# Hybrid decoder trunk on one core: sums of down-projection weight blocks formed by adding DMA transfers instead of VectorE

## The chip, the cores and the metric

One Trainium2 chip, one core of it. The metric is the device time of one launch in microseconds (us). The kernel before takes 1595.86 us, the median of three runs that lie between 1595.35 and 1596.35 us.

## The reference, cut to what matters

Two layers of a decoder trunk over 512 tokens of width 1024. The change is in the second half of each layer, the MLP:

```python
for l in range(DEPTH):                      # DEPTH = 2
    ...                                     # norm, projections, conv / gated linear attention / window attention, w_o
    h = rms_norm(x, norm2_w[l])
    x = x + jnp.square(jax.nn.relu(h @ w_up[l])) @ w_down[l]     # w_up (1024, 4096), w_down (4096, 1024)
```

All is float32. The output is x, (1, 512, 1024).

## The kernel before, in words

**Precision by splitting.** Each operand of a TensorE product is kept as a high part (rounded by ScalarE) and a low part (what is left, by VectorE), and each product is three matmuls: high by high, high by low, low by high. A *unit* is a block of weights, 128 x 1024 numbers, that is split so: `split_high` (ScalarE, L803 to L820, 128x1024 copy), then `split_low` (VectorE, L1037 to L1045). There are four buffers for split units (`SPLIT = 4`), so the split of unit n waits until TensorE has finished unit n-4 (`unit_done`, L816).

**The MLP.** It runs in four quarters of 1024 hidden columns. A quarter is eight units `up` (hidden = up projection, ReLU and square on ScalarE) and then fourteen units `dn` (down projection). The down projection of a quarter is a product of a 512x1024 and a 1024x1024 matrix, each seen as 2x2 blocks: Strassen's scheme in Winograd's form, seven block products instead of eight, from sums of blocks of the hidden values and sums of blocks of w_down. Each product is two units: `pair` 0 and 1 are two halves of its 512 contraction rows, so `dn(14q + 2*place + pair)` is one unit, of twelve matmuls 128x512. The seven products run in the order `PRODUCT = (0, 4, 5, 2, 3, 1, 6)`: place 0 is product 0, place 1 is product 4, and so on.

**The weight blocks.** For each pair the blocks b11, b12, b21, b22 of a quarter (128 x 1024 numbers each, 512 KB) are loaded into a buffer `down[pair]` (`raw_down`) by two DMAs issued by SyncE (L493), and `down_full[pair]` says that they are there. VectorE then forms the sums in place, four instructions for each pair and quarter, `ta`, `tb`, `tc`, `td`: b12 = b22 - b12 (L1493), b11 = b12 + b11 (L1495), b22 = b22 - b11 (L1499), b21 = b21 - b11 (L1497). `split_high` of a unit waits for the sum that it reads (L811). Each sum overwrites a block whose earlier value must have been split before. Products 0, 1 and 5 read blocks as loaded. When the last of a quarter's units of a pair are split, `down_free[pair]` allows SyncE to load the next quarter.

**Order of the work.** The four engines' orders in the MLP are lists written out: `PE_LATE`, `ACT_LATE` (ScalarE) and `DVE_LATE` (VectorE); a word with `+` is the split of a unit, `rs` takes a product out of PSUM, `fo` folds sums of products into x, `su`/`sh`/`sl`, `df`/`dh`/`dl` and `hh`/`hl` prepare the hidden values, `RM` is the norm's factors, `ra`, `rb` add the w_o product. Every engine works through its list strictly in order. GpSimd has no block in this kernel. After the last quarter, layer 1's first steps (`UT4` to `UT7`: transposes of x on TensorE; `gq0`, `gq1`, `gk0`) follow in the same lists, and after layer 1 the output is stored.

The sums of products g1, g5, g6, g7 (`product_sums`, L1415, L1417) collect over the quarters; `fold` (L1419 to L1430) and `scaled_into_x` (L1395) bring them into x with the factor `rsq2`.

Of the kernel before, what the change touches and what calls it, by code (L numbers as in the profile page):

```python
# [10 lines left out]
P = 128  # L11
# [78 lines left out]
ACT_LATE = """+wa3 +wb0 +wb1 V0 +wb2 +wb3 V1 V2 V3 +up0 +up1 sq0 +up2 V4 V5 sq1 V6 +up3 V7 sq2 sq3 +up4 rl0 rl1 hh0 +up5 +up6 rl2  # L90
hh1 hh2 rl3 +up7 dh0 rl4 +dn0 hh3 sh0 hh4 rl5 +dn1 hh5 rl6 sh1 +dn2 hh6 rl7 +dn3 sh2 sh3 +dn4 +dn5 hh7 +dn6 +dn7 +dn8
+dn9 +dn10 +dn11 +dn12 +dn13 +up8 +up9 +up10 +up11 rl8 hh8 +up12 rl9 rl10 hh9 +up13 hh10 +up14 rl11 +up15 hh11 dh1
rl12 +dn14 hh12 sh4 +dn15 rl13 hh13 rl14 sh5 +dn16 sh6 rl15 +dn17 +dn18 sh7 hh14 +dn19 +dn20 hh15 +dn21 +dn22 +dn23
+dn24 +dn25 +dn26 +dn27 +up16 +up17 +up18 +up19 rl16 +up20 hh16 rl17 rl18 hh17 hh18 +up21 +up22 +up23 rl19 hh19 dh2
rl20 +dn28 sh8 hh20 +dn29 rl21 sh9 rl22 hh21 +dn30 hh22 rl23 +dn31 +dn32 sh10 +dn33 sh11 +dn34 +dn35 +dn36 +dn37 +dn38
+dn39 hh23 +dn40 +dn41 +up24 +up25 +up26 rl24 +up27 hh24 rl25 hh25 +up28 +up29 +up30 rl26 rl27 hh26 +up31 hh27 dh3
rl28 +dn42 hh28 sh12 rl29 +dn43 hh29 sh13 +dn44 rl30 hh30 sh14 rl31 +dn45 hh31 sh15 +dn46 +dn47 +dn48 +dn49 +dn50
+dn51 +dn52 +dn53 +dn54 +dn55 +gq0 UT4 +gq1 UT5 UT6 +gk0 UT7""".split()


DVE_LATE = """+wa3 ra0 +wb0 ra1 +wb1 ra2 ra3 V0 +wb2 +wb3 V1 +up0 V2 +up1 V3 rb0 ta0 rb1 rb2 +up2 rb3 +up3 V4 V5 V6 V7 +up4 RM hl0
+up5 +up6 ta1 df0 +up7 hl1 hl2 dl0 su0 +dn0 tb0 hl3 hl4 su1 +dn1 hl5 tb1 su2 +dn2 sl0 sl1 su3 hl6 +dn3 sl2 rs0 +dn4
rs1 sl3 +dn5 +dn6 rs2 td0 +dn7 rs3 +dn8 td1 rs5 rs4 +dn9 rs6 rs7 hl7 +dn10 tc0 +dn11 rs8 +dn12 tc1 rs9 +dn13 rs10 +up8
+up9 +up10 +up11 rs11 rs13 hl8 ta2 rs12 +up12 +up13 ta3 hl9 df1 hl10 +up14 +up15 dl1 su4 +dn14 hl11 tb2 +dn15 sl4 hl12
tb3 su5 hl13 su6 +dn16 sl5 sl6 su7 +dn17 +dn18 td2 rs15 rs14 +dn19 sl7 td3 +dn20 rs16 rs17 hl14 rs18 +dn21 rs19 +dn22
hl15 +dn23 +dn24 rs21 rs20 tc2 rs22 +dn25 tc3 +dn26 rs23 +dn27 +up16 rs24 rs25 rs27 +up17 ta4 rs26 +up18 +up19 ta5
hl16 +up20 hl17 hl18 +up21 +up22 df2 +up23 hl19 dl2 su8 sl8 +dn28 tb4 su9 +dn29 tb5 su10 sl9 hl20 hl21 hl22 +dn30 su11
+dn31 sl10 +dn32 rs29 +dn33 rs28 td4 sl11 rs30 +dn34 +dn35 rs31 rs33 rs32 td5 +dn36 +dn37 +dn38 rs35 rs34 tc4 +dn39
hl23 tc5 rs36 +dn40 rs37 +dn41 rs38 +up24 +up25 rs39 +up26 fo7 ta6 rs41 +up27 rs40 +up28 fo6 hl24 +up29 +up30 hl25 ta7
df3 +up31 hl26 hl27 dl3 su12 +dn42 hl28 sl12 tb6 su13 +dn43 sl13 tb7 +dn44 su14 hl29 hl30 sl14 su15 +dn45 hl31 sl15  # L110
rs42 rs43 +dn46 fo1 +dn47 rs44 rs45 +dn48 td6 +dn49 td7 rs46 +dn50 +dn51 rs47 rs49 +dn52 +dn53 tc6 rs48 fo3 fo4 fo2
rs50 rs51 tc7 +dn54 fo0 +dn55 UT4 +gq0 rs52 UT5 UT6 rs53 UT7 +gq1 fo5 rs54 rs55 +gk0""".split()
# [89 lines left out]
def hybrid_trunk(nc, x, x_cols, positions, params, w_in, gla_wa2, w_branch, w_o, w_up, w_down, norms, consts, gmask, out):  # L202
# [3 lines left out]
    with ctx:  # L206
# [101 lines left out]
        rsq2 = after("rsqrt_tokens_mlp_sq", [TT])  # L308
        ident, ones = cst[:, 0:P], cst[:, CC["ones"]:CC["ones"] + 1]
# [10 lines left out]
        def sem(name):  # L320
            return ctx.enter_context(nc.semaphore(name))
# [9 lines left out]
        down_free = [sem(f"down_free{i}") for i in range(PAIRS)]  # L331
        acc_free = [sem(f"acc_free{i}") for i in range(4)]
# [7 lines left out]
         diff_ready, b12_summed, b11_summed, b21_summed, b22_summed, angle_ready, sines_ready, first_full, first_hi, first_lo) = map(sem, """  # L340
# [6 lines left out]
         diff_ready b12_summed b11_summed b21_summed b22_summed angle_ready sines_ready first_full first_hi first_lo""".split())  # L347
# [442 lines left out]
        def _(act):  # L790
# [69 lines left out]
            for l in range(DEPTH):  # L860
# [125 lines left out]
                for word in ACT_LATE:  # L986
# [16 lines left out]
                    elif kind == "rl":  # L1003
                        a, free = done(act, l, f"up{i}")
                        nc.scalar.activation(hid[:, k, :], a[:], ACT.Relu).then_inc(free, 1)  # L1005
                        nc.scalar.drain()
                        nc.scalar.activation(hid[:, k, :], hid[:, k, :], ACT.Square).then_inc(hid_val, 1)
                    elif kind == "hh":
                        if k < BK:
                            nc.scalar.activation(h11[0][:, k, :], hid[:, k, 0:2 * P], ACT.Copy).then_inc(hid_hi, 1)  # L1010
                        else:
                            nc.scalar.activation(h2[0][:, k - BK, :], hid[:, k, :], ACT.Copy).then_inc(hid_hi, 1)
                    elif kind == "dh":
                        act.wait_ge(diff_val, l * QUARTERS + i + 1)
                        nc.scalar.activation(hd[0][:], hd_sum[:], ACT.Copy).then_inc(diff_hi, 1)
                    elif kind == "sh":
                        act.wait_ge(sums_val, l * QUARTERS * BK + i + 1)
                        nc.scalar.activation(hs[0][:, i % BK], hs_sum[:, i % BK], ACT.Copy).then_inc(sums_hi, 1)


        @block.vector
        def _(dve):
# [120 lines left out]
            for l in range(DEPTH):  # L1143
# [249 lines left out]
                def scaled_into_x(row, t, half, part):  # L1393
                    x_at = x_tok[:, 2 * row + t, half * SEQ:(half + 1) * SEQ]
                    return V.scalar_tensor_tensor(out=x_at, in0=part, scalar=rsq2[:, 2 * row + t:2 * row + t + 1], in1=x_at,  # L1395
# [23 lines left out]
                def fold(i):  # L1419

                    g1, g6, g5, g7 = (g[:] for g in gsum)
                    if i == 1:
                        V.tensor_tensor(g6, g6, g1, ALU.add)
                    elif i == 3:
                        V.tensor_tensor(g7, g7, g6, ALU.add)
                    else:
                        row, half, part = {0: (0, 0, g1), 2: (0, 1, g6), 4: (1, 1, g7), 5: (1, 0, g7),
                                           6: (0, 1, g5), 7: (1, 1, g5)}[i]
                        for t in range(2):
                            scaled_into_x(row, t, half, part[:, t, :])  # L1430

                for word in DVE_LATE:
# [21 lines left out]
                    elif kind == "RM":  # L1454
                        row_norm(2 * l + 1, rsq2[:])
                        V.tensor_tensor(rsq2[:], rsq2[:], rsq2[:], ALU.mult)
                    elif kind == "hl":
# [8 lines left out]
                    elif kind == "df":  # L1466
                        dve.wait_ge(hid_val, (l * QUARTERS + i) * 8 + BK)
                        V.tensor_tensor(hd_sum[:], hid[:, 0:BK, 0:2 * P], hid[:, 0:BK, 2 * P:],
# [4 lines left out]
                    elif kind == "su":  # L1473
# [13 lines left out]
                    elif kind in ("ta", "tb", "tc", "td"):  # L1487
                        n, pair = l * QUARTERS + i // 2, i % 2
                        b11, b12 = down[pair][:, :, 0, 0:SEQ], down[pair][:, :, 0, SEQ:]
                        b21, b22 = down[pair][:, :, 1, 0:SEQ], down[pair][:, :, 1, SEQ:]  # L1490
                        if kind == "ta":
                            dve.wait_ge(down_full[pair], (n + 1) * 32)
                            V.tensor_tensor(b12, b22, b12, ALU.subtract).then_inc(b12_summed, 1)  # L1493
                        elif kind == "tb":
                            V.tensor_tensor(b11, b12, b11, ALU.add).then_inc(b11_summed, 1)  # L1495
                        elif kind == "tc":
                            V.tensor_tensor(b21, b21, b11, ALU.subtract).then_inc(b21_summed, 1)  # L1497
                        else:
                            V.tensor_tensor(b22, b22, b11, ALU.subtract).then_inc(b22_summed, 1)  # L1499
# [57 lines left out]
```

## Time and profile before

| | |
|---|---|
| runs | 1595.86 us median (1595.35 to 1596.35) |
| the profiled execution | 1595.84 us, of which the span from the first to the last instruction is 1594.0 us |
| TensorE (PE) busy | 1568.7 us, 98% |
| VectorE (DVE) busy | 1077.5 us, 68% |
| ScalarE (ACT) busy | 743.9 us, 47% |
| GpSimd (POOL) busy | 0.2 us |
| mean DMA rate | 96 GB/s, 153.23 MB in all |

PE is TensorE's matmuls, PEld its weight loads. An engine's busy time says little of what ends last; the waits of PE do, since PE is nearly always at work. Matmuls overlap in the records (one lasts 0.39 us and the next starts 0.23 us after it), so a pause between records is a little shorter than the time that is lost. SPq, DVEq mean the instruction queue of an engine (DMA issues, drains, semaphores).

### The profile page before, as it was taken

How to read it: one execution, taken by the hardware profiler on the slowest of the kernel's cores; microseconds unless marked ns; L12 is line 12 of the kernel's file. 1: busy time of each engine (PE TensorE's matmuls, PEld its weight loads, DVE VectorE, ACT ScalarE, POOL GpSimd, SP SyncE). 2: the span in 40 equal slices, each digit the busy share in tenths (PEclk: the TensorE clock that was granted, in tenths of full speed). 3: DMA queues.
4: the chain of work that ended last, by engine and by line, in shares of the span. 5: the costliest groups of instructions: out<-in, count | busy, mean ns of one | idle time of the engine just before them, and what ended most of it. 6: DMA issues, size and time to landing. Idle time of an engine off the chain costs nothing.

```text
span 1594.0 us, 21259 instructions
## 1 busy us (share of the span) xinstructions
PE 1568.7 (98%) x7528; PEld 1283.7 (81%) x7528; DVE 1077.5 (68%) x1511; ACT 743.9 (47%) x1131; POOL 0.2 (0%) x4
## 2 busy tenths in 40 slices
PE   8999999999999999999999999999999999999997
PEld 7877778888888888888777787788888888888885
DVE  5577764555458878687966777555455586877788
ACT  5657552323247363636345566422232563636361
POOL 0000000000000000000000000000000000000000
PEclk9999999999999999999999999999999999999999
DMA  7321312332261322323023212133323514141401
GB/s 230 105 80 55 96 63 80 106 114 98 79 212 53 139 73 100 112 105 112 1 82 103 81 54 80 54 106 113 99 80 106 185 53 159 54 158 53 159 1 53
DMA packets 109321, 153.23 MB, mean 96 GB/s; under 512 B 5120, under 2 KB 81440, under 8 KB 109216
## 3 DMA queue, kind: packets, MB, share of 16 engines
q1 hardware_dynamic: 108496, 151.27, 28.7%
q8 instruction: 60, 0.98, 0.2%
q10 hardware_dynamic: 720, 0.61, 0.1%
q14 instruction: 45, 0.37, 0.1%
HBM read 149.77 MB, written 2.10 MB: 95 GB/s over the span
## 4 chain that ended last, share of the span: by engine, by line
PE 86%; DVE 9%; ACT 2%; DVEq 1%; issue 1%; DMA 1%; SPq 0%; ACTq 0%
PE acc L538 18%; PE acc L539 18%; PE acc L540 18%; PE acc L589 5%; PE acc L590 5%; PE acc L591 5%; PE acc L560 4%; PE acc L562 4%; PE acc L561 4%; DVE wl_rows L1042 3%; DVE x_tokens L1395 1%; PE bank L726 1%; PE bank L745 1%; PE bank L737 1%; DMA raw<-in_w_in_dram 1%
## 5 line engine op out<-in xcount | busy, mean ns | idle before, releaser
L538 PE MATMUL acc<-uh,wh 128*128 128x512 f32 x1152 | 453.5, 394 | 6.4 <-DVEq L1136 4.5
L540 PE MATMUL acc<-uh,wl 128*128 128x512 f32 x1152 | 449.3, 390 | 0.0
L539 PE MATMUL acc<-ul,wh 128*128 128x512 f32 x1152 | 449.3, 390 | 0.0
L538 PEld LDWEIGHTS acc<-uh,wh 128*128 128x128 f32 x1152 | 216.7, 188 | 58.1 <-issue 5.6
L540 PEld LDWEIGHTS acc<-uh,wl 128*128 128x128 f32 x1152 | 216.7, 188 | 45.9
L539 PEld LDWEIGHTS acc<-ul,wh 128*128 128x128 f32 x1152 | 216.9, 188 | 43.7
L1042 DVE TENSOR_TENSOR wl<-raw,wh 128x1024 fp32r<-128x1024 f32 x142 | 174.0, 1225 | 73.1 <-ACT wh L820 61.1
L820 ACT ACTIVATE wh<-raw 128x1024 fp32r<-128x1024 f32 x142 | 150.6, 1060 | 134.8 <-PE acc L540 98.0
L820 ACT ACTIVATE wh_rows<-raw_down 128x1024 fp32r<-128x1024 f32 x112 | 118.9, 1062 | 155.5 <-DVE raw_down L1497 66.7
L1042 DVE TENSOR_TENSOR wl_rows<-raw_down,wh_rows 128x1024 fp32r<-128x1024 f32 x112 | 137.2, 1225 | 11.1 <-ACT wh_rows L820 1.1
L1072 DVE TENSOR_TENSOR gate_tanh<-acc,rsqrt_rows 128x512 f32<-128x512 f32 x48 | 33.2, 691 | 116.6 <-PE acc L540 116.4
L980 ACT ACTIVATE gate_tanh<-gate_tanh 128x512 f32<-128x512 f32 x40 | 25.3, 633 | 171.7 <-DVEq L1073 171.7
L560 PE MATMUL acc<-wh_rows,uh 128*128 128x512 f32 (+1 forms) x256 | 96.0, 375 | 0.6 <-DVE gla_a_tokens L1165 0.6
L562 PE MATMUL acc<-wl_rows,uh 128*128 128x512 f32 (+1 forms) x256 | 93.4, 365 | 0.0
L561 PE MATMUL acc<-wh_rows,ul 128*128 128x512 f32 (+1 forms) x256 | 93.3, 364 | 0.0
L589 PE MATMUL acc<-wh_rows,hidden_hi 128*128 128x512 f32 x192 | 75.7, 394 | 7.4 <-DVE wl_rows L1042 5.0
L1005 ACT ACTIVATE hidden<-acc 128x512 f32<-128x512 f32 x64 | 38.3, 599 | 95.0 <-PE acc L540 93.3
L589 PE MATMUL acc<-wh_rows,hidden_sums_hi 128*128 128x512 f32 x192 | 75.1, 391 | 0.3 <-DVE x_tokens L1395 0.3
L590 PE MATMUL acc<-wh_rows,hidden_lo 128*128 128x512 f32 x192 | 75.2, 392 | 0.0
L591 PE MATMUL acc<-wl_rows,hidden_hi 128*128 128x512 f32 x192 | 75.2, 392 | 0.0
L590 PE MATMUL acc<-wh_rows,hidden_sums_lo 128*128 128x512 f32 x192 | 74.8, 389 | 0.0
L591 PE MATMUL acc<-wl_rows,hidden_sums_hi 128*128 128x512 f32 x192 | 74.7, 389 | 0.0
(227 smaller groups left out, 2378.9 us busy)
## 6 DMA issues: line engine op xcount, KB each, us to landing
raw<-in_w_in_dram SPq DMA_DIRECT2D x39, 1024.0 KB, 5.2
raw<-in_w_up_dram SPq DMA_DIRECT2D x32, 1024.0 KB, 5.6
raw_down<-in_w_down_dram SPq DMA_DIRECT2D x32, 1024.0 KB, 8.2
raw_branch<-in_w_in_dram SPq DMA_DIRECT2D x12, 1024.0 KB, 5.0
raw_branch<-in_w_branch_dram SPq DMA_DIRECT2D x12, 1024.0 KB, 5.1
raw_branch<-in_w_o_dram SPq DMA_DIRECT2D x8, 1024.0 KB, 5.0
x_tokens<-in_x_dram SPq DMA_DIRECT2D x8, 256.0 KB, 8.2
raw_kv<-in_w_in_dram SPq DMA_DIRECT2D x4, 512.0 KB, 4.9
```

Source lines behind the costliest of these rows:

```text
L538: nc.tensor.matmul(a[:], wh[slot][:, k, :], right_h, start=at_k == 0, stop=False)
L539: nc.tensor.matmul(a[:], wh[slot][:, k, :], right_l, start=False, stop=False)
L540: last = nc.tensor.matmul(a[:], wl[slot][:, k, :], right_h, start=False, stop=at_k == n - 1)
L560: nc.tensor.matmul(to, left_h[:, k, s], h[:, row, 0:cols], start=k == 0, stop=False)
L561: nc.tensor.matmul(to, left_l[:, k, s], h[:, row, 0:cols], start=False, stop=False)
L562: last = nc.tensor.matmul(to, left_h[:, k, s], lo[:, row, 0:cols], start=False, stop=k == KT - 1)
L589: nc.tensor.matmul(to[:], left[0], h[:, row, :], start=k == 0, stop=False)
L590: nc.tensor.matmul(to[:], left[1], h[:, row, :], start=False, stop=False)
L591: last = nc.tensor.matmul(to[:], left[0], lo[:, row, :], start=False, stop=k == BK - 1)
L820: nc.scalar.activation(split_view(True, u, l), raw_view(u), ACT.Copy).then_inc(hi_done, 1)
L1005: nc.scalar.activation(hid[:, k, :], a[:], ACT.Relu).then_inc(free, 1)
L1042: V.tensor_tensor(split_view(False, u, l), raw_view(u), split_view(True, u, l).bitcast(f32), ALU.subtract).then_inc(lo_done, 1)
```

## The change

The eight VectorE sums of a quarter (`ta`, `tb`, `tc`, `td` for both pairs, 64 instructions in all) are removed. GpSimd gets a block of its own that issues eight DMA transfers a quarter, each of which adds its source (512 KB) to a block in `down[pair]`: b12 += b22 on landing; b11 += b12 as stored in w_down in DRAM, once product 0's unit has been split; b12 += b11 from DRAM, once product 4's unit has been split; b12 += b21, once product 2's unit has been split. The first and the last read SBUF, the other two DRAM. Each transfer has its own semaphore, and `split_high` waits for that. The transfers only add, so the signs of some block sums are turned, of the hidden values' too (`df`, `su`), and one fold takes the factor `-rsq2` (`rsq2_minus`, computed once a layer in `RM`). `down_block` names the blocks anew. The lists `ACT_LATE` and `DVE_LATE` are written anew; `PE_LATE` and the loads by SyncE are as they were.

```diff
-        down_block: row, col = ((0, 0), (1, 0), (0, 0), (1, 1), (0, 1), (1, 1), (1, 0))[product]
+        down_block: row, col = ((0, 0), (1, 0), (0, 1), (0, 0), (0, 1), (1, 1), (0, 1))[product]
...
-                        act.wait_ge({2: b11_summed, 3: b22_summed, 4: b12_summed, 6: b21_summed}[i],
-                                    2 * (l * QUARTERS + q) + pair + 1)
+                        act.wait_ge({2: sum_2_full, 3: sum_1_full, 4: sum_3_full, 6: sum_4_full}[i][pair],
+                                    16 * (l * QUARTERS + q + 1))
...
+        @block.gpsimd
+        def _(pool):
+            for l in range(DEPTH):
+                for q in range(QUARTERS):
+                    n = l * QUARTERS + q
...
+                    def top(pair, half):
+                        first = q * D_MODEL + 2 * pair * P
+                        return w_down[l, first:first + 2 * P, half * SEQ:(half + 1) * SEQ].rearrange("(k p) n -> p k n", p=P)
+
+                    def split_by(place, pair):
+                        pool.wait_ge(lo_done, unit_at(l, f"dn{14 * q + 2 * place + pair}") + 1)
+
+                    for pair in range(PAIRS):
+                        b11, b12, b21, b22 = blocks(pair)
+                        pool.wait_ge(down_full[pair], (n + 1) * 32)
+                        pool.dma_start(b12, b22, accum_op=ALU.add).then_inc(sum_3_full[pair], 16)
+                    for pair in range(PAIRS):
+                        b11, b12, b21, b22 = blocks(pair)
+                        split_by(PLACE[0], pair)
+                        pool.dma_start(b11, top(pair, 1), accum_op=ALU.add).then_inc(sum_1_full[pair], 16)
+                    for pair in range(PAIRS):
+                        b11, b12, b21, b22 = blocks(pair)
+                        split_by(PLACE[4], pair)
+                        pool.dma_start(b12, top(pair, 0), accum_op=ALU.add).then_inc(sum_2_full[pair], 16)
+                    for pair in range(PAIRS):
+                        b11, b12, b21, b22 = blocks(pair)
+                        split_by(PLACE[2], pair)
+                        pool.dma_start(b12, b21, accum_op=ALU.add).then_inc(sum_4_full[pair], 16)
...
-                    elif kind in ("ta", "tb", "tc", "td"):
-                        ...
-                            V.tensor_tensor(b12, b22, b12, ALU.subtract).then_inc(b12_summed, 1)
-                        ...
-                            V.tensor_tensor(b11, b12, b11, ALU.add).then_inc(b11_summed, 1)
-                        ...
-                            V.tensor_tensor(b21, b21, b11, ALU.subtract).then_inc(b21_summed, 1)
-                        ...
-                            V.tensor_tensor(b22, b22, b11, ALU.subtract).then_inc(b22_summed, 1)
...
+                        V.drain()
+                        V.tensor_scalar(rsq2_minus[:], rsq2[:], -1.0, None, ALU.mult)
```

Below, sum 3, sum 1, sum 2 and sum 4 are the four transfers in the order in which GpSimd issues them: sum 3 feeds product 4 (`dn2`, `dn3` of a quarter), sum 2 product 2 (`dn6`, `dn7`), sum 1 product 3 (`dn8`, `dn9`), sum 4 product 6 (`dn12`, `dn13`).

## Rows read from the trace of the kernel before

**Rows 1.** The page, its first part: the span and TensorE's busy time.
```profile
span 1594.0 us, 21259 instructions
...
PE 1568.7 (98%) x7528; PEld 1283.7 (81%) x7528; DVE 1077.5 (68%) x1511; ACT 743.9 (47%) x1131; POOL 0.2 (0%) x4
```

**Rows 2.** Stretches of product units: from:to length, busy us (count) by engine, clock, DMA share, GB/s.
```profile
508.50:546.60 38.10, 38.10 (x169) 31.44 (x168) 34.37 (x37) 18.43 (x19) 0.00 (x0) 1.00 0.14 55
...
754.60:797.70 43.10, 39.50 (x180) 31.79 (x179) 39.38 (x44) 18.56 (x20) 0.00 (x0) 1.00 0.00 1
...
1544.90:1594.00 49.10, 39.10 (x163) 30.98 (x161) 41.74 (x47) 13.71 (x14) 0.00 (x0) 0.95 0.12 43
```

**Rows 3.** Waits of PE, 728 to 815 us: who for whom, us in total, times, longest.
```profile
PE bank L606 <- DVEq L1411: 1.7, 1, 1.7
...
PE acc L589 <- DVE product_sums L1417: 1.2, 1, 1.2
...
PE acc L589 <- DVE wl_rows L1042: 0.7, 1, 0.7
...
PE acc L538 <- DVEq L1063: 1.0, 1, 1.0
PE acc L538 <- DVE wl L1042: 0.6, 2, 0.4
PE bank L606 <- DVEq L1406: 0.5, 1, 0.5
```

**Rows 4.** Waits of PE, 1518 to 1594 us.
```profile
PE acc L589 <- DVE wl_rows L1042: 4.3, 1, 4.3
...
PE acc L589 <- DVE x_tokens L1395: 0.3, 1, 0.3
```

**Rows 5.** PE's timeline behind the longest pause (start, us, what), and a stretch's clock.
```profile
1582.76 0.80 PE L589 MATMUL acc<-wh_rows,hidden_hi 128*128 128x512 f32 x1 [4.32 <-DVE wl_rows L1042]
...
1585.80 0.40 PE L590 MATMUL acc<-wh_rows,hidden_lo 128*128 128x512 f32 x1
...
1582.00:1586.00 4.00, 3.24 (x8) 2.61 (x9) 3.65 (x5) 0.48 (x1) 0.00 (x0) 0.57 0.07 26
```

**Rows 6.** VectorE's groups that the change touches, and a wait on them in the whole trace.
```profile
L1493 DVE TENSOR_TENSOR raw_down<-raw_down 128x1024 f32<-128x1024 f32 x16 | 19.6, 1226 | 14.8 <-DMA raw_down<-in_w_down_dram 13.2 <-issue 0.9
...
L1456 DVE TENSOR_TENSOR rsqrt_tokens_mlp_sq<-rsqrt_tokens_mlp_sq 128x4 f32<-128x4 f32 x2 | 0.3, 164 | 0.1
...
ACT wh_rows L820 <- DVE raw_down L1497: 66.7, 16, 8.5
```

**Rows 7.** VectorE's timeline, low splits of dn0 to dn3 in the first quarter.
```profile
496.39 1.23 DVE L1042 TENSOR_TENSOR wl_rows<-raw_down,wh_rows 128x1024 fp32r<-128x1024 f32 x1
...
501.85 1.22 DVE L1042 TENSOR_TENSOR wl_rows<-raw_down,wh_rows 128x1024 fp32r<-128x1024 f32 x1
...
507.14 1.23 DVE L1042 TENSOR_TENSOR wl_rows<-raw_down,wh_rows 128x1024 fp32r<-128x1024 f32 x1
...
512.86 1.23 DVE L1042 TENSOR_TENSOR wl_rows<-raw_down,wh_rows 128x1024 fp32r<-128x1024 f32 x1
```

**Rows 8.** PE's timeline: first matmul of dn0 and of dn2, first quarter.
```profile
508.70 0.39 PE L589 MATMUL acc<-wh_rows,hidden_hi 128*128 128x512 f32 x1
...
514.14 0.39 PE L589 MATMUL acc<-wh_rows,hidden_diff_hi 128*128 128x512 f32 x1
```

**Rows 9.** DMA issues: KB each, median us to landing; last, raw_kv's 512 KB loads.
```profile
raw<-in_w_in_dram SPq DMA_DIRECT2D x39, 1024.0 KB, 5.2
...
raw_down<-in_w_down_dram SPq DMA_DIRECT2D x32, 1024.0 KB, 8.2
...
DMA to landing us min/median/max: 3.6/4.9/6.6
```

More of the change, by code:

```diff
@@ L87 @@
 dn45 dn46 dn47 dn48 dn49 dn50 dn51 dn52 dn53 UT4 UT5 UT6 UT7 dn54 dn55""".split()
[L90 to L98, printed above, removed]
@@ L101 @@
[L101 to L110, printed above, removed]
@@ L111 @@
-rs42 rs43 +dn46 fo1 +dn47 rs44 rs45 +dn48 td6 +dn49 td7 rs46 +dn50 +dn51 rs47 rs49 +dn52 +dn53 tc6 rs48 fo3 fo4 fo2
-rs50 rs51 tc7 +dn54 fo0 +dn55 UT4 +gq0 rs52 UT5 UT6 rs53 UT7 +gq1 fo5 rs54 rs55 +gk0""".split()
+ACT_LATE = """+wa3 +wb0 V0 +wb1 +wb2 +wb3 V1 V2 +up0 +up1 +up2 V3 V4 sq0 V5 +up3 sq1 sq2 sq3 V6 V7 rl0 +up4 +up5 rl1 hh0 +up6 rl2
+hh1 +up7 rl3 dh0 hh2 +dn0 rl4 sh0 hh3 +dn1 rl5 hh4 +dn2 rl6 sh1 rl7 hh5 +dn3 hh6 +dn4 sh2 sh3 +dn5 +dn6 +dn7 hh7 +dn8
++dn9 +dn10 +dn11 +dn12 +dn13 +up8 +up9 rl8 +up10 rl9 +up11 +up12 hh8 hh9 +up13 rl10 +up14 hh10 +up15 rl11 +dn14 dh1
@@ new lines @@
++dn52 +dn53 +dn54 +dn55 UT4 UT5 +gq0 UT6 +gq1 +gk0 UT7""".split()
+DVE_LATE = """+wa3 ra0 +wb0 ra1 ra2 ra3 V0 +wb1 +wb2 +wb3 V1 +up0 +up1 V2 rb0 rb1 V3 rb2 +up2 rb3 +up3 V4 V5 V6 V7 +up4 +up5 hl0
++up6 RM df0 dl0 +up7 hl1 su0 +dn0 +dn1 hl2 hl3 sl0 hl4 su1 +dn2 su2 sl1 su3 +dn3 +dn4 sl2 rs0 hl5 sl3 rs1 +dn5 rs3
++dn6 rs2 +dn7 +dn8 hl6 rs4 +dn9 rs5 +dn10 rs6 hl7 rs7 rs8 +dn11 +dn12 +dn13 rs9 rs10 +up8 +up9 rs12 rs11 +up10 +up11
+rs13 hl8 +up12 hl9 +up13 df1 +up14 +up15 +dn14 su4 hl10 su5 sl4 dl1 +dn15 hl11 hl12 +dn16 su6 sl5 su7 hl13 +dn17 rs14
@@ L114 @@
++dn45 sl15 +dn46 rs42 +dn47 rs43 +dn48 fo0 rs45 +dn49 rs44 hl31 +dn50 rs46 +dn51 fo1 +dn52 rs49 rs48 rs47 fo3 fo2 fo4
++dn53 rs50 +dn54 rs51 rs52 +dn55 UT4 UT5 rs53 +gq0 +gq1 UT6 UT7 fo5 rs54 rs55 +gk0""".split()
 SLAB = {}
@@ L308, in hybrid_trunk @@
         rsq2 = after("rsqrt_tokens_mlp_sq", [TT])
+        rsq2_minus = after("rsqrt_tokens_mlp_sq_minus", [TT])
         ident, ones = cst[:, 0:P], cst[:, CC["ones"]:CC["ones"] + 1]
@@ L331, in hybrid_trunk @@
         down_free = [sem(f"down_free{i}") for i in range(PAIRS)]
+        sum_3_full = [sem(f"sum_3_full{i}") for i in range(PAIRS)]
+        sum_1_full = [sem(f"sum_1_full{i}") for i in range(PAIRS)]
+        sum_2_full = [sem(f"sum_2_full{i}") for i in range(PAIRS)]
+        sum_4_full = [sem(f"sum_4_full{i}") for i in range(PAIRS)]
         acc_free = [sem(f"acc_free{i}") for i in range(4)]
@@ L346, in hybrid_trunk @@
          x_summed u_hi u_ready hid_val hid_hi hid_ready sums_val sums_hi sums_ready diff_val diff_hi
-         diff_ready b12_summed b11_summed b21_summed b22_summed angle_ready sines_ready first_full first_hi first_lo""".split())
+         diff_ready angle_ready sines_ready first_full first_hi first_lo""".split())
         UNIT_CREDIT = SPLIT
@@ L376, in down_block @@
             product, d = PRODUCT[i % PRODUCTS], down[pair]
-            row, col = ((0, 0), (1, 0), (0, 0), (1, 1), (0, 1), (1, 1), (1, 0))[product]
+            row, col = ((0, 0), (1, 0), (0, 1), (0, 0), (0, 1), (1, 1), (0, 1))[product]
             return d[:, :, row, col * SEQ:(col + 1) * SEQ]
@@ L1018, in _, with blocks @@
                         nc.scalar.activation(hs[0][:, i % BK], hs_sum[:, i % BK], ACT.Copy).then_inc(sums_hi, 1)
+        @block.gpsimd
[3 more added lines that the diff above has]
+                    n = l * QUARTERS + q
+                    def blocks(pair):
+                        d = down[pair]
+                        return d[:, :, 0, 0:SEQ], d[:, :, 0, SEQ:], d[:, :, 1, 0:SEQ], d[:, :, 1, SEQ:]
+                    def top(pair, half):
[19 more added lines that the diff above has]
+                        pool.dma_start(b12, b21, accum_op=ALU.add).then_inc(sum_4_full[pair], 16)
         @block.vector
@@ L1391, in _, with scaled_into_x @@
                     V.drain().then_inc(down_free[pair], 1)
-                def scaled_into_x(row, t, half, part):
+                def scaled_into_x(row, t, half, part, factor=rsq2):
                     x_at = x_tok[:, 2 * row + t, half * SEQ:(half + 1) * SEQ]
-                    return V.scalar_tensor_tensor(out=x_at, in0=part, scalar=rsq2[:, 2 * row + t:2 * row + t + 1], in1=x_at,
+                    return V.scalar_tensor_tensor(out=x_at, in0=part, scalar=factor[:, 2 * row + t:2 * row + t + 1], in1=x_at,
                                                   op0=ALU.mult, op1=ALU.add)
@@ L1429, in fold @@
                         for t in range(2):
-                            scaled_into_x(row, t, half, part[:, t, :])
+                            scaled_into_x(row, t, half, part[:, t, :], rsq2_minus if i == 5 else rsq2)
                 for word in DVE_LATE:
```

28 lines of the change are left out of this document (15 added, 13 removed).

## The prediction

> **What bounds the kernel now.** I read the page's first part, then PE's waits, then the busy times of the stretches in which the change works. PE is busy for 1568.7 of 1594.0 us [rows 1], so everything that the change can give lies in PE's idle 25 us, and only in the part of it that VectorE causes in the MLP. The stretches of product units tell where that is: in the first quarter PE is busy for 38.10 of 38.10 us, though VectorE works 34.37 of them, and the six quarters that are not the last of a layer all look like this; in the last quarter of layer 0 it is 39.50 of 43.10, in that of layer 1 39.10 of 49.10 [rows 2] (of the latter some 4 us are the tail behind the last matmul, in which x is finished and stored). So VectorE is close to its limit in every product stage, but it is late only in the last quarter of each layer, where the folds into x come on top. PE's waits there: 1.7, 1.2, 0.7, 1.0, 0.6 and 0.5 us in layer 0 [rows 3] and 4.3, 1.2 and 0.3 us in layer 1 [rows 3, 4] (the line of the 1.2 reads alike in both layers and stands once, in the first group). All end at VectorE. ScalarE waits for the block sums for long (66.7 us in 16 waits for one of the four [rows 6]), but what that does to PE is already in those few waits.
>
> **What is removed.** 64 instructions of 128x1024 (four lines, 16 times each, one of them shown), 1.226 us each [rows 6]: 78.5 us of VectorE, 9.8 us a quarter. In six of eight quarters PE doesn't wait for VectorE in the product stage, so there this gives nothing. Their waits for landing, 13.2 us in all [rows 6], go with them and gave nothing either. In the two last quarters VectorE runs out of time by the sum of PE's waits, at most 5.8 us, and is relieved of nearly twice that. So I let these waits go:
> - Layer 0, products and the transposes among them: 1.7 + 1.2 + 0.7 = 3.6 us [rows 3].
> - Layer 1: 4.3 + 1.2 + 0.3 = 5.8 us [rows 3, 4].
> - The records draw a matmul until 0.39 us after its start, while the next can start after 0.227 (twelve matmuls a unit: 514.14 - 508.70 is two units, so one unit is 2.72 us [rows 8]). Each of the six waits thus costs 0.16 us more than it shows: 1.0 us.
> - After the 4.3 us pause PE works at the lower level for a while: clock 0.57 on average in the 4 us stretch; seven starts take 1585.80 - 1582.76 = 3.04 us instead of 7 x 0.227 = 1.59 [rows 5]. That is 1.4 us, which goes with the pause.
>
> Sum: 3.6 + 5.8 + 1.0 + 1.4 = 11.8 us. Not taken: the waits 1.0, 0.6 and 0.5 in layer 0 [rows 3], 2.1 us with 0.6 for four pauses. They stand in the passage to layer 1, where VectorE follows PE's last products (x finished, transposed, split) and PE has little else to do; less load on VectorE may shorten them, so they set the lower end. The tail behind the last matmul is the same chain as before and stays.
>
> **What is added to VectorE, ScalarE.** Two instructions on 128x4, by the neighbouring line 0.16 us each with a drain [rows 6], in `RM`, early in the MLP, where PE is covered: nothing. Turned signs cost nothing: the operations on the hidden values have the same count and shape. ScalarE's waits for VectorE's sums become waits for DMAs. Behind such a wait on ScalarE's list stand the next splits and the `hh` copies; behind these VectorE's low splits; behind these PE. So the question is only whether the sums land in time.
>
> **What is added to the DMAs.** 64 transfers of 512 KB. Sum 3 starts when the blocks land, tens of us before product 4 needs it: the loads of a quarter are in before the last `up` units. Sum 1 starts when dn0 and dn1 are split, some 11 and 6 us before dn0 even begins, and is needed for dn8, eight units later. Sum 4 starts when dn6 is split and has six units. Sum 2 is the tight one: it waits for the split of dn2 and dn3 and feeds dn6 and dn7, four units later. In the first quarter the low splits of dn0 to dn3 end at 497.6, 503.1, 508.4 and 514.1 us [rows 7]. dn0 starts on PE at 508.70, so dn6 starts at 508.70 + 6 x 2.72 = 525.0 and dn7 at 527.7 [rows 8]. Before that a unit needs its high split, as long as PE's buffers allow, and its low split of 1.23 us [rows 7]; I set 2.4 us for both. Sum 2 must then have landed by 522.6 (pair 0) and 525.3 (pair 1): 14.2 and 11.2 us after its start, if it starts at once. But sums 1 and 2 of both pairs, four transfers, are issued between 497.6 and 514.1. If the queue serves one after the other and each takes S, the fourth lands at 497.6 + 4S when S is above some 5.5, and is in time up to S = (525.3 - 497.6)/4 = 6.9 us. The other quarters have nearly the same spacing, and their PE time line is the same to 0.1 us.
>
> **What S is.** No row shows a transfer that adds, nor one issued from GpSimd; the bounds are the nearest rows. Below: plain loads of 512 KB land in 3.6, 4.9 and 6.6 us (least, median, most) [rows 9], and an adding transfer reads its target besides. Above: read, read and write as if it were three plain passes, 1.5 MB, by the 5.2 us of a 1 MB load: 7.8 us [rows 9]; by the w_down loads, which go in twos at 8.2 us for 2 MB, 6.2 us. And with no upper end by reason, since an adder inside the DMA path may have a rate of its own, and GpSimd may write its descriptors slowly; no row speaks of either. I take 5.2 us, the 1 MB load, since two reads of 512 KB are nearest to it. Then sum 2 lands at 513.6 and 519.3: no wait reaches PE, and the cost is nothing. The cover is the 6 to 9 us by which the splits are ahead of PE; beyond S = 6.9 it is used up in all eight quarters alike, at 4 x (S - 6.9) us each.
>
> The Trainium skill, DMA: Bandwidth & Descriptors, "Anatomy of one DMA", gives an accumulating transfer no price; its fit for plain ones issued from GpSimd is 2.0 us plus bytes over 436 GB/s, by which one pass of 512 KB is an estimated 3.2 us and three are 5.6 us, so the sum by it would be the same. No run here shows it yet.
>
> The added traffic is 33.5 MB on a mean rate that leaves the DMAs at a 0.14 share in a product stage [rows 2]; SyncE's loads of the next `up` units fall into it, but with one of two slabs always ahead. I take nothing for that.
>
> **Forecast.** 1595.8 - 11.8 = 1584.0 us, the profiled execution being as long as the median.
>
> **The rivals.**
> - *The sums land late.* The place is sum 2 of pair 1 (and pair 0 from S = 8.3): ScalarE stands at the split of dn6 or dn7, VectorE behind it, PE behind both. It costs 8 x 4 x (S - 6.9). It decides from 32 x (S - 6.9) = 11.8, S = 7.3 us. S = 8 gives 1584.0 + 35 = 1619 us, S = 9 1651 us, S = 10 1683 us. For it: an addition is unknown in this trace and my own upper bound, 7.8, lies beyond 7.3. Against: DMA share of 0.14, so no one else is in the way, and the w_down price of 6.2. Chance 0.25 for S up to 10.
> - *GpSimd can't write the descriptors beside a busy VectorE.* In a product stage VectorE works 34.37 of 38.10 us [rows 2] with pauses of 0.1 us; if GpSimd could issue only in the pauses, each sum would come some VectorE instructions late, S above 10, and the time above 1683 us. The trace has no GpSimd work beside VectorE. All VectorE instructions of rows 6 and 7 take 1.2 ns an element with two SBUF inputs. Chance 0.08. The Trainium skill, SBUF — State Buffer, box "The 'DVE blocks DMA' trap (SWDGE)", says just this: while VectorE runs in a mode that takes the shared port pair, GpSimd can't write descriptors; by it, one transfer of 620 ns took 3100 ns. It limits this to fast modes of VectorE, and the rows here show none, so by that page as I read it the case doesn't arise.
> - *The waits only change their name.* In the last quarter the order of folds, `rs` steps and transposes on VectorE stays, and a wait of 1.2 us for `product_sums` [rows 3, 4] may be a place in the list and not a lack of time; the 0.7 and 4.3 us for a low split may come back as waits for sum 4. Then 2 to 4 us remain of the gain: 1592 to 1594 us, about no change. Chance 0.10.
> - *The change doesn't do what it says*: a transfer that is issued far later than the split that frees its block, since GpSimd's list is in order too: sum 1 of pair 0 stands behind sum 3 of pair 1, which waits for the second load. That load lands before the last `up` units, so no. It is held in the first rival.
>
> **How the numbers follow.** Forecast 0.57, late sums 0.25, descriptors 0.08, no change 0.10. The lower end of the range is the forecast with the 2.7 us of the passage and a little of the tail gone too: 1580 us. The upper end must take in most of the late sums: S = 8.6 gives 1584.0 + 32 x 1.7 = 1638; some 0.15 lies above. Within 0.2% (3.2 us, about what a measurement of this kernel can tell from no change) lies half of the third rival and the narrow strip of S around 7.3: 0.07. Slower: 0.25 + 0.08 less that strip: 0.31. Faster: 0.62. The forecast's own range is 1580 to 1590 us.
>
> **What would show each step.** Right: no PE wait in 755 to 798 and in the last 50 us beyond some tenths; VectorE busy 78 us less; ScalarE's waits for the sums' DMAs short; issue to landing of the sums below 7 us, with sum 2 of pair 1 below 11. Wrong: PE waits in the middle of every product stage, before dn6 or dn7, that end at a low split whose high split waited for a DMA from GpSimd; then S is what I mis-sized. If all sums land in time and PE still waits in the last quarters, the step from VectorE's load to its lateness was wrong. A descriptor jam would show as a long gap between the split and the first packet of the sum; a slow adder as packets that last long.

## The result, and the profile after

The changed kernel takes 1601.76 us, the median of five runs (1599.55 to 1604.15); the kernel before, beside it, 1595.6 us. The ratio is 1.0038, with a 95% interval of 1.0023 to 1.0052: slower by 0.4%, where 0.7% faster was forecast. Its own runs lie 4.6 us apart, those of before 1.0 us. The profiled execution is the slowest of them (1604.15 us, span 1602.4 us), so its waits add up to a little more than the median's.

The page of the changed kernel, first part; the line of DMA traffic, the new queue, and the issues of the sums with their median landing time:

```profile
span 1602.4 us, 21199 instructions
...
PE 1574.2 (98%) x7528; PEld 1286.8 (80%) x7528; DVE 998.9 (62%) x1449; ACT 743.6 (46%) x1131; POOL 78.3 (5%) x68
...
DMA packets 126729, 186.79 MB, mean 117 GB/s; under 512 B 6144, under 2 KB 82464, under 8 KB 126624
...
q0 software_dynamic: 17408, 33.56, 13.1%
...
raw_down<-raw_down POOLq DMA_DIRECT2D x32, 512.0 KB, 5.8
raw_down<-in_w_down_dram POOLq DMA_DIRECT2D x32, 512.0 KB, 6.3
```

VectorE is relieved of 1077.5 - 998.9 = 78.6 us [rows 1], as summed. But PE's waits have not gone, they have moved. All waits of PE in the changed kernel (who for whom, us in total, times, longest), the first lines:

```profile
PE acc L593 <- DVE product_sums L1456: 10.1, 4, 4.0
PE acc L593 <- DVE x_tokens L1434: 4.2, 6, 1.0
PE acc L542 <- DVEq L1175: 3.7, 1, 3.7
...
PE acc L593 <- DVE wl_rows L1081: 0.7, 2, 0.5
```

L593 is the first matmul of a triple in a product, L589 before. The 4.3 us behind a low split [rows 4] are gone, and the 1.7 us before a transpose of x [rows 3] are down to 0.3. In their place PE waits for VectorE to read a finished product out of PSUM (L1456, L1434), and not in the last quarters alone. The product stages of layer 1's first and second quarter (from:to length, busy us and count of PE, PEld, DVE, ACT, POOL, clock, DMA share, GB/s):

```profile
1301.30:1341.40 40.10, 38.90 (x169) 31.25 (x168) 31.09 (x36) 18.63 (x20) 4.88 (x4) 1.00 0.56 122
1384.90:1427.40 42.50, 40.05 (x170) 32.63 (x169) 30.82 (x36) 17.35 (x18) 4.87 (x4) 0.96 0.50 109
```

Such a stage took 38.10 us with PE always busy [rows 2]; now 40.1 and 42.5 us, though VectorE works 3 us less in it. The chain behind the second of these losses, on ScalarE, VectorE and PE (start, us, engine, line, what, idle before and what ended it):

```profile
1402.07 3.44 ACT L824 ACTIVATE wh_rows<-raw_down 128x1024 fp32r<-128x1024 f32 x3 [5.44 <-DMA raw_down<-in_w_down_dram]
```
```profile
1403.16 1.22 DVE L1081 TENSOR_TENSOR wl_rows<-raw_down,wh_rows 128x1024 fp32r<-128x1024 f32 x1 [3.35 <-ACT wh_rows L824]
1404.48 0.69 DVE L1456 TENSOR_TENSOR product_sums<-product_sums,acc 128x512 f32<-128x512 f32 x1
```
```profile
1405.22 0.50 PE L593 MATMUL acc<-wh_rows,hidden_sums_hi 128*128 128x512 f32 x1 [2.45 <-DVE product_sums L1456]
```

Read from the top: ScalarE stands 5.44 us before the high split of dn21 (sum 2 of pair 1), until the transfer lands; VectorE stands 3.35 us before its low split; behind that, in VectorE's list, is the `rs` step that frees an accumulator, and PE waits 2.45 us for it. After the pause PE is at the lower of its two levels (1.2 GHz) for a while: granted clock 0.60 in 1405 to 1409 us, and 0.57 in 1573 to 1577 us after the longest pause, of 4.0 us.

Why the transfer lands so late stands on GpSimd's timeline, first quarter of layer 0 of the changed kernel. The first two lines are sum 1, the next two sum 2, the last two sum 4, each for pair 0 and 1:

```profile
499.33 1.22 POOL L1049 DMA_DIRECT2D raw_down<-in_w_down_dram  x1 [26.01 <-DVE wl_rows L1081]
505.52 1.23 POOL L1049 DMA_DIRECT2D raw_down<-in_w_down_dram  x1 [4.98 <-issue]
512.12 1.21 POOL L1053 DMA_DIRECT2D raw_down<-in_w_down_dram  x1 [5.36 <-issue]
518.67 1.22 POOL L1053 DMA_DIRECT2D raw_down<-in_w_down_dram  x1 [5.34 <-issue]
526.22 1.22 POOL L1057 DMA_DIRECT2D raw_down<-raw_down  x1 [6.33 <-issue]
531.60 1.22 POOL L1057 DMA_DIRECT2D raw_down<-raw_down  x1 [4.16 <-issue]
```

The first waits for its split. All the others wait for "issue": nothing that the profile shows. They start 6.2 to 7.6 us apart behind a transfer from DRAM and 5.4 us apart behind one within SBUF, and by the landing times in the trace each starts 0.32 us after the one before has landed. So do 38 of the 64 transfers of this run, all 32 of sums 2 and 4 among them. Issue to landing is 6.3 us in the median for sums 1 and 2 and 5.1 for sum 4; the 5.8 above mixes sum 4 with sum 3, which takes 7.9. Is that room, is it the speed of the adding transfers, or are the new lists to blame anyway? The experiments take these apart.

### The profile page after: what moved, and what is told of

It is laid out like the page before. It is cut to its first block, busy times and chain, and to the rows that moved or that the text cites. A ratio compares the mean times of both kernels' runs of the same rounds, so it can differ in the third digit from the quotient of the medians.

```text
span 1602.4 us, 21199 instructions
## 1 busy us (share of the span) xinstructions
PE 1574.2 (98%) x7528; PEld 1286.8 (80%) x7528; DVE 998.9 (62%) x1449; ACT 743.6 (46%) x1131; POOL 78.3 (5%) x68
## 4 chain that ended last, share of the span: by engine, by line
PE 86%; DVE 7%; DMA 2%; ACT 2%; issue 1%; DVEq 1%; ACTq 0%
PE acc L542 19%; PE acc L543 19%; PE acc L544 19%; PE acc L564 4%; PE acc L566 4%; PE acc L565 4%; PE acc L593 4%; PE acc L594 4%; PE acc L595 4%; DVE wl_rows L1081 3%; DMA raw_down<-in_w_down_dram 2%; DVE x_tokens L1434 1%; PE bank L730 1%; ACT wh_rows L824 1%; PE bank L749 1%
## 5 line engine op out<-in xcount | busy, mean ns | idle before, releaser
L824 ACT ACTIVATE wh_rows<-raw_down 128x1024 fp32r<-128x1024 f32 x112 | 118.9, 1061 | 135.3 <-DMA raw_down<-in_w_down_dram 61.8
L593 PE MATMUL acc<-wh_rows,hidden_sums_hi 128*128 128x512 f32 x192 | 78.3, 408 | 14.9 <-DVE product_sums L1456 10.1
L593 PE MATMUL acc<-wh_rows,hidden_hi 128*128 128x512 f32 x192 | 74.9, 390 | 0.0
```

What stands on the lines that cost most here:

```text
L593: nc.tensor.matmul(to[:], left[0], h[:, row, :], start=k == 0, stop=False)
```

## The experiments

Each ran beside the kernel before on the same chip; ratios are to that one.

**Twice the room for descriptors.**

```diff
-    nc = _bacc.Bacc("TRN2", target_bir_lowering=False, num_devices=1, dynamic_dma_scratch_size=1024)
+    nc = _bacc.Bacc("TRN2", target_bir_lowering=False, num_devices=1, dynamic_dma_scratch_size=2048)
```

> The changed kernel with one number changed: the space reserved for GpSimd's DMA descriptors (dynamic_dma_scratch_size) 2048 instead of 1024 bytes a partition. In the changed kernel GpSimd begins each transfer of a burst only about when the one before has landed (499.3, 505.5, 512.1, 518.7 us). Theory A, space for descriptors holds the next one back: the fourth transfer of a burst is issued as soon as its split allows, 2 to 5 us earlier, sum 2 of pair 1 lands earlier by as much, PE's waits in the product stages (17 us in all) go, and the time is 1584 to 1588 us. Theory B, the transfers themselves take turns (the adding path is busy for 5 to 6 us with each): issued earlier, they land as late as before, issue to landing grows from 6.3 to 9 us and more, time 1600 us. Theory C, the new lists of VectorE and ScalarE cause the waits, whatever the transfers do: 1600 us with nothing changed in the landing times.

Measured: 1583.99 us (1583.61 to 1584.38), ratio 0.9926 (0.9911 to 0.9941). Theory A holds. GpSimd's timeline in the same quarter:

```profile
499.51 1.21 POOL L1049 DMA_DIRECT2D raw_down<-in_w_down_dram  x1 [26.18 <-DVE wl_rows L1081]
502.08 1.23 POOL L1049 DMA_DIRECT2D raw_down<-in_w_down_dram  x1 [1.37 <-DVE wl_rows L1081]
507.79 1.21 POOL L1053 DMA_DIRECT2D raw_down<-in_w_down_dram  x1 [4.47 <-DVE wl_rows L1081]
513.84 1.20 POOL L1053 DMA_DIRECT2D raw_down<-in_w_down_dram  x1 [4.84 <-DVE wl_rows L1081]
523.62 1.21 POOL L1057 DMA_DIRECT2D raw_down<-raw_down  x1 [8.58 <-DVE wl_rows L1081]
525.78 1.22 POOL L1057 DMA_DIRECT2D raw_down<-raw_down  x1 [0.95 <-DVE wl_rows L1081]
```

No more "issue": each transfer now waits for its split alone, and sum 2 of pair 1 starts at 513.84 instead of 518.67 us. Two transfers overlap (499.51 and 502.08) and land 2.6 us apart, and issue to landing stays 6.3 us in the median for sum 1 and 6.1 for sum 2. So the adding path can take a second transfer long before the first has landed; theory B, turns of 5 to 6 us in the path itself, falls. Of all waits of PE in this run, one line lies in the product stages:

```profile
PE acc L593 <- DVE x_tokens L1434: 2.5, 2, 1.3
```

**No sums at all.**

```diff
-        @block.gpsimd
-        def _(pool):
-            ...
-                    if i in (0, 1, 5):
-                        act.wait_ge(down_full[pair], (l * QUARTERS + q + 1) * 32)
-                    else:
-                        act.wait_ge({2: sum_2_full, ...}[i][pair], 16 * (l * QUARTERS + q + 1))
+                    act.wait_ge(down_full[pair], (l * QUARTERS + q + 1) * 32)
```

> The changed kernel without any of its 64 transfers: GpSimd has no work, every split of a dn unit waits for the load alone, and the sums of weight blocks are left out. Lists, signs and everything else as in the changed kernel. It gives what relieving VectorE is worth when no sum is ever late. Theories A and B (late sums are the whole loss): no PE wait of over 1 us in any product stage, 1582 to 1586 us. Theory C (the lists): waits for product_sums and x_tokens stay, 1598 to 1602 us.

Measured: 1583.88 us (1583.85 to 1584.16), ratio 0.9926 (0.9911 to 0.994). Theory C falls: with the same lists and no late sum there is no loss. (What a late sum costs does depend on the lists, as the point on the limit shows below.) It also bounds what better transfers can give: with room they cost 0.1 us.

**Plain copies.**

```diff
-                        pool.dma_start(b12, b22, accum_op=ALU.add).then_inc(sum_3_full[pair], 16)
+                        pool.dma_start(b12, b22).then_inc(sum_3_full[pair], 16)
```

and the other three likewise.

> The changed kernel with its 64 transfers as plain copies instead of additions (the sums of weight blocks are left out, each transfer overwrites its target); still issued from GpSimd at the same places. It prices the addition. If adding is the cost (the target is read too, an adder's rate): issue to landing falls from 6.3 and 5.1 us to 4 us or less, the spacing of a burst from 6.6 to below 5 us, and the time to about 1586 us. If the path through GpSimd is the cost (descriptors, 1.2 us an issue, completion): landing stays within 1 us of 6.3 and the time near 1598 us.

Measured: 1583.81 us. By the time the first expectation holds, and landing takes 4.4 us from DRAM and 3.2 within SBUF, where 4 or less was expected; the trace says what an addition costs. Sum 1's line in this run, with least, median and most from issue to landing under it:

```profile
L1049 POOL DMA_DIRECT2D raw_down<-in_w_down_dram x16: 722/722/731, 499.0 to 1529.7; - x16
...
DMA to landing us min/median/max: 4.1/4.4/6.1
```

With the addition, in the run with 2048 bytes:

```profile
L1049 POOL DMA_DIRECT2D raw_down<-in_w_down_dram x16: 1208/1222/1234, 499.5 to 1530.3; - x16
...
DMA to landing us min/median/max: 6.1/6.3/8.0
```

So the addition costs 1.9 us from issue to landing, 0.5 of them in GpSimd's issue (0.72 to 1.22 us). The plain copies were issued at once even with 1024 bytes (501.59 us for the second): two of them had room. Why, this run alone doesn't tell; that a copy needs less room than an addition, which also reads its target, is argued.

**Another order.**

```diff
-                    (both pairs: sum 1; then both pairs: sum 2)
+                    for number, pair in ((1, 0), (2, 0), (2, 1), (1, 1)):
+                        split_by(PLACE[0] if number == 1 else PLACE[4], pair)
+                        ...
```

> The changed kernel with GpSimd's list in another order: sum 1 of pair 0, sum 2 of pair 0, sum 2 of pair 1, sum 1 of pair 1 (before: both sum 1, then both sum 2). Sum 2 of pair 1 is then third in the burst, and sum 1 of pair 1 (needed for dn9, two units later) fourth. Theories A and B alike: sum 2 lands 5 to 6 us earlier for pair 1, the PE waits in the middle of the product stages go or shrink below 1 us, time 1585 to 1590 us. Theory C: 1600 us.

Measured: 1594.52 us (1592.54 to 1597.67, ten runs), ratio 0.9992 (0.9983 to 1.0001): 7 us better than the changed kernel, not the 12 to 17 expected. The lateness is handed on. ScalarE's waits for transfers from DRAM, 61.8 us in all in the changed kernel, are here 24.8 for sum 2 and 32.6 for sum 1, and 29.5 for sum 4. PE waits 4.1 us at most. With one transfer at a time, six of them (four of 6.5 and two of 5.4 us, 37 us) fill a product stage of 38 us, so another order can hardly make them all early (argued; this one order was run).

**How much room, and what for.**

```diff
-dynamic_dma_scratch_size=1024
+dynamic_dma_scratch_size=1536
```

> The changed kernel with 1536 bytes for GpSimd's DMA descriptors (1024 as it is: 1601.8 us; with 2048: 1584.0 us). If what matters is that two of these transfers find room side by side, and that two need only a little more than 1024 bytes, 1536 is as good as 2048: each transfer issued as its split allows, 1583 to 1586 us. If more than 1536 bytes are needed for two, it stays at 1598 to 1604 us with spacings of 6.3 to 6.7 us in a burst.

Measured: 1583.98 us (1583.71 to 1584.26), ratio 0.9925 (0.9911 to 0.994). 1536 bytes are as good as 2048. Two adding transfers are in flight here, and a third is not let in. Twice in this run a third comes due (675.35 and 1460.19 us), and both start 0.3 us after the first of the two in flight has landed; one is put down to "issue":

```profile
1460.19 1.21 POOL L1053 DMA_DIRECT2D raw_down<-in_w_down_dram  x1 [1.65 <-issue]
```

With 2048 bytes the same transfer starts at 1459.56 us, as the third in flight.

```diff
-                        pool.dma_start(b12, b22, accum_op=ALU.add).then_inc(sum_3_full[pair], 16)
+                        for k in range(2):
+                            pool.dma_start(b12[:, k], b22[:, k], accum_op=ALU.add).then_inc(sum_3_full[pair], 16)
```

and the other three likewise, at 1024 bytes.

> The changed kernel (1024 bytes) with each transfer cut in two of 256 KB, issued one behind the other, so 128 transfers of half the descriptors. If the room in bytes is the limit (theory A): three halves fit at a time, GpSimd may issue the next sum's first half while the last half is still under way, so that sums follow each other 1 to 3 us closer than the 6.5 us before, and the time falls, to 1586 to 1596 us. If GpSimd simply allows one sum's transfers at a time, or the limit is a number of transfers, then halves gain nothing or cost 1 to 2 us a sum for the second issue: 1602 us and more.

Measured: 1584.48 us (1584.03 to 1584.7), ratio 0.9928 (0.9913 to 0.9943), better than expected. GpSimd's timeline, start of the same quarter:

```profile
499.61 1.78 POOL L1051 DMA_DIRECT2D raw_down<-in_w_down_dram  x2 [24.40 <-DVE wl_rows L1085]
502.13 0.86 POOL L1051 DMA_DIRECT2D raw_down<-in_w_down_dram  x1 [0.74 <-DVE wl_rows L1085]
505.60 0.88 POOL L1051 DMA_DIRECT2D raw_down<-in_w_down_dram  x1 [2.61 <-issue]
```

Three halves are issued without a hitch, the fourth waits 2.61 us for room. A limit on the number of transfers in flight would be one here and three there; a limit in room fits both. How the room is given back is more than a count of bytes, and no run shows it: the fourth half starts 0.33 us after the second has landed (505.27 us), 2.3 us after the first. So twice the transfers of half the size need no more room and give back all but 0.5 us.

**A control.** The kernel before with 2048 bytes:

> A control: the kernel before with 2048 instead of 1024 bytes of descriptor space, which moves all its buffers by 1024 bytes and changes nothing else, since it issues no DMA from GpSimd. Theory A: no effect, 1595.9 us within 0.2%. If the gain of the run with 2048 bytes were due to where the buffers lie, this kernel would gain too, some 12 us.

Measured: 1596.08 us, ratio 1.0 (0.9991 to 1.001). Where the buffers lie changes nothing in this kernel, and the halves gain at 1024 bytes, with every buffer where it was.

**Where VectorE's relief is worth something.** Two runs leave sums out of the kernel before, with its lists otherwise kept; the words `ta` to `td` of the quarters in question go, and their splits wait for the load.

```diff
-                    if i in (0, 1, 5):
+                    if i in (0, 1, 5) or q == QUARTERS - 1:
                         act.wait_ge(down_full[pair], (l * QUARTERS + q + 1) * 32)
```

> The kernel before, its lists and signs kept, with VectorE's 16 sums of weight blocks in the last quarter of each layer (8 a layer) left out altogether, so that the product there uses unsummed blocks; the 48 sums in the other quarters stay. The prediction put the whole gain of relieving VectorE, 11.8 us, into these two quarters. If so: 1584 to 1587 us. If the order of VectorE's list in the last quarter is the cause and not its load, PE's waits there stay: 1593 us and more.

Measured: 1587.17 us (1586.79 to 1587.61), ratio 0.9945 (0.993 to 0.996).

> The complement: the kernel before with the 48 sums of the first three quarters of each layer left out, and the last quarter's 16 kept. PE never waits in the product stages of those quarters, so relieving VectorE there is worth nothing: 1596 us within 0.1%. If VectorE carries a backlog from one quarter into the last, it gains some us.

Measured: 1595.58 us, ratio 0.9998 (0.9989 to 1.0008). 16 instructions in two quarters are worth 9.0 us, 48 in the other six at most the 0.6 us by which the medians differ. What is left of the 12 us, 3 us, is put down to the new lists by elimination; no run has them alone. Without the last quarter's sums PE still waits for a low split and for the passage to layer 1:

```profile
PE acc L591 <- DVE wl_rows L1044: 2.1, 1, 2.1
...
PE acc L540 <- DVEq L1065: 1.0, 1, 1.0
PE bank L608 <- DVEq L1413: 0.8, 1, 0.8
```

With the new lists and room (2048 bytes), PE's waits between 757 and 803 us are 1.3, 0.3 and 0.2 us.

**Transfers in the last quarter only.**

```diff
-                for q in range(QUARTERS):
+                for q in (QUARTERS - 1,):
...
+                        if kind == "ta":
+                            V.tensor_tensor(b12, b12, b22, ALU.add).then_inc(sum_3_full[pair], 1)
+                        elif kind == "tb":
+                            V.tensor_tensor(b12, b12, b11, ALU.add).then_inc(sum_2_full[pair], 1)
+                        elif kind == "tc":
+                            V.tensor_tensor(b11, b12, b22, ALU.subtract).then_inc(sum_1_full[pair], 1)
+                        else:
+                            V.tensor_tensor(b12, b12, b21, ALU.add).then_inc(sum_4_full[pair], 1)
```

> With 2048 bytes: the changed kernel, but in the first three quarters of each layer VectorE forms the sums again (24 instructions a layer, 1.23 us each; ta before the up units' last splits, tb behind the split of dn2 and dn3, tc behind dn4 and dn5, td behind dn6 and dn7), and only in the last quarter do the transfers. The prediction said that relieving VectorE is worth something only in the last quarter of a layer. If so, this is as fast as all four quarters by DMA, 1583 to 1586 us. If the relief in the other quarters is worth something with these lists, PE waits for product_sums or low splits there and the time is above 1588 us.

Measured: 1625.93 us (1625.48 to 1627.8), ratio 1.0187 (1.017 to 1.0204). A clear miss. The waits that the second expectation named are there, but the run doesn't test what it was meant to: with the turned signs `tb` can come only behind the split of dn2, and I put all of `tb`, `tc` and `td` right behind splits of the product stage. PE's waits in 505 to 720 us there:

```profile
PE acc L597 <- DVE product_sums L1461: 5.4, 3, 2.6
PE acc L597 <- DVE product_sums L1463: 5.0, 3, 3.1
PE acc L597 <- DVE wl_rows L1088: 2.3, 3, 1.0
PE acc L597 <- DVE hidden_sums_lo L1533: 2.1, 1, 2.1
PE acc L597 <- DVE x_tokens L1441: 1.3, 1, 1.3
```

It shows that in the other quarters VectorE has little slack in the product stage (34 of 38 us [rows 2]): the sums fit in where the list before had them, and not where I put them. The question itself was answered by leaving sums out, above.

**Room and order.**

> The changed kernel with 2048 bytes for the descriptors and, besides, sum 2 issued before sum 1 of pair 1. With the room alone 1584.0 us. There only 7.1 us in 3 waits of ScalarE end at sum 2, and none reaches PE, so the order can give nothing more: 1583.5 to 1584.5 us.

Measured: 1583.99 us (1583.52 to 1584.75), ratio 0.9926 (0.9911 to 0.9941). As expected: once there is room, the order is nothing. The run also shows what a close overlap costs. Sum 1, with the issue time under which it is listed, and least, median and most from issue to landing:

```profile
L1050 POOL DMA_DIRECT2D raw_down<-in_w_down_dram x16: 1208/1468/1722, 499.0 to 1543.1; - x16
...
DMA to landing us min/median/max: 6.0/8.0/9.1
```

The eight of pair 1 start 0.73 us after sum 2 of pair 1, land 8.0 to 9.1 us after their start, and 2.5 to 2.8 us after that sum 2.

## Why the prediction was wrong, point by point

The step that failed is the one that put the cost of the transfers at nothing ("no wait reaches PE, and the cost is nothing"). The sums land late with 1024 bytes, one after the other, and that costs 17.8 us (1601.76 against 1583.99 us with room for two), more than the gain of 11.8 that the rest of the sum forecast. Two parts of the step were wrong: S, and the limit up to which a late sum costs nothing.

- **The bound, and what the relief is worth: right, in part by luck.** The forecast of 1584.0 us was that of transfers that land in time. With room for two it is 1583.99, without sums 1583.88. The place was right too: 9.0 us in the two last quarters, at most 0.6 in the six others. The step "the passage waits stay" was too careful and another too generous: in the passage to layer 1 the waits shrink from 2.1 [rows 3] to 0.4 us, while waits of 1.3 us for x stay in both last quarters. By layer the forecast had 4.1 and 7.7 us; from the first product of a layer on, the profiled execution with 2048 bytes gains 5.3 us in layer 0 (first products of the two layers at 508.80 and 1293.37 us, before at 508.70 and 1298.60) and 6.5 in layer 1. The errors cancel in the sum.
- **S, the time of a transfer: mis-sized.** I took 5.2 us, the 1 MB load [rows 9]. Issue to landing is 6.3 us from DRAM and 5.1 within SBUF, and the start-to-start distance behind a transfer from DRAM in a burst 6.2 to 7.9 us. The bounds, 3.6 to 7.8 us, held it.
- **One after the other: priced, but without a cause.** The formula 497.6 + 4S is what happens with 1024 bytes, from 499.3 us on and with 6.6 us for S in the first burst (the landing and 0.32 us). I left it open as a property of a queue and looked for no cause. The cause is the room that the kernel's own line sets: with more of it the same additions on the same queue overlap.
- **The limit of 6.9 us: wrong by more than S.** With S = 6.5, four transfers end at 26.0 us, within my 27.7 us, and PE should never have waited. Two things made the limit shorter. The first transfer starts at 499.3 and not at 497.6 us. In the first quarter sum 2 of pair 1 so lands at 525.9 us, 0.6 behind my 525.3, and PE waits 0.5 us before dn7, and 0.6 and 0.5 us more for the x steps (L1434) that stand behind it on VectorE. And I counted up to the split of dn7, as if only that unit waited for it. On VectorE the `rs` steps that free accumulators stand behind the low split, and PE needs those earlier: in the second quarter of layer 1 sum 2 of pair 1 landed 0.5 us later than the limit that I would set (1384.93 + 7 x 2.72 - 2.4 = 1401.6; the split began at 1402.07), and PE lost 2.45 us in the middle of dn20, and more by the lower clock after it. In the second and the last quarter of layer 0 it landed 1.0 and 0.7 us before that limit (608.29 and 773.04 us), and PE waited all the same:

```profile
611.47 0.50 PE L593 MATMUL acc<-wh_rows,hidden_sums_hi 128*128 128x512 f32 x1 [0.98 <-DVE product_sums L1456]
...
776.30 0.47 PE L593 MATMUL acc<-wh_rows,hidden_sums_hi 128*128 128x512 f32 x1 [2.67 <-DVE product_sums L1456]
```

The order of the new `DVE_LATE` explains where these waits are. It has `+dn21 rs17` and `+dn49 rs44`, where the list before had both `rs` ahead of that split (`rs17 hl14 rs18 +dn21`, `rs44 rs45 +dn48 td6 +dn49`); `rs17` frees the accumulator for the second half of dn20, `rs44` the one for dn48. All four waits for L1456, 10.1 us, lie in these two quarters of the two layers. In the first and third quarters the list has both `rs` ahead of the split of pair 1, and PE never waits for them. That the changed kernel would lose less at 1024 bytes with these two words moved is argued; no run has it. I named this queue in the prediction ("behind these VectorE's low splits; behind these PE") and left it out of the sum.
- **The rivals.** Late sums was the right one, at the place that I named (sum 2 of pair 1). Its price, 8 x 4 x (S - 6.9), has the wrong zero, and it has all quarters alike. The loss against 1584 is 17.8 us, 2.2 us a quarter in the mean and very uneven: against the profiled execution with 2048 bytes, that of the changed kernel (20.1 us longer) loses 2.5, 1.3, 0.0 and 4.3 us in the quarters of layer 0 and 2.1, 4.4, 0.1 and 5.6 in those of layer 1, each from its first product to that of the next, or to the end. Descriptors blocked by a busy VectorE: no. GpSimd's issue of sums 1, 2 and 4 takes 1.20 to 1.23 us beside a VectorE that is busy for 31 of 40 us, with hardly any spread (1208 to 1234 ns for sum 1 with room, above). The Trainium skill, SBUF — State Buffer, box "The 'DVE blocks DMA' trap (SWDGE)", limits that trap to VectorE's fast modes; this agrees with it. The waits that only change their name: partly, 1.3 us for x in each last quarter.
- **Range and chances.** 1601.8 us lies inside 1580 to 1638 us; the sign of the forecast was wrong, with 0.31 on the side that came.

The Trainium skill, DMA: Bandwidth & Descriptors, section "SWDGE vs HWDGE vs iDMA", says that GpSimd appends its descriptors to rings in a reserved part of SBUF. The traces fit a wait for room in them: GpSimd stands still between issues at 1024 bytes, up to 6.7 us, once for 1.65 us at 1536, and never at 2048.

## What to carry to other kernels

Before work is handed to DMAs from GpSimd, look at `dynamic_dma_scratch_size`: if GpSimd's issues follow each other at just the landing time of a transfer and their wait is "issue", they lack room, and 512 bytes a partition more, or transfers of half the size, gave it here (17.8 and 17.3 us). A time limit for a late buffer ends at the first thing that is queued behind the waiting instruction on every engine down the line, not at the unit that reads the buffer; so a list written for sums that are never late decides what a late one costs. Work that is taken off an engine is worth what the bound engine waits for it, in the stages where it does: here 16 of 64 instructions carried 9.0 of the 12 us, and the other 48 at most 0.6.

## What the runs showed of the hardware that was not expected

- With 1024 bytes of descriptor space one adding transfer of 512 KB (256 rows of 2 KB) is in flight at a time, with 1536 two, with 2048 at least three; of halves with 128 rows three fit in 1024. One that has to wait for room starts 0.3 us after one in flight has landed.
- An addition in a transfer costs 1.9 us more from issue to landing than a plain copy of the same 512 KB (6.3 against 4.4 us from DRAM, 5.1 against 3.2 us within SBUF), and 0.5 us more of GpSimd (1.22 against 0.72 us).
- Adding transfers overlap, but none lands sooner than 2.5 us after the one before it in the runs with room (1536 and 2048 bytes, 512 KB each), and no half of 256 KB sooner than 1.25 us. One that starts 2.6 us after another takes 6.3 us as if alone, one that starts 0.73 us after it takes 8.0 to 9.1.
